# A mixture-of-experts decoder step on one core: routing moved into the experts' stage, slot tables built by matrix products

## What is computed

```
scores = sigmoid(x @ router_w)            # 1088 x 16 experts
sel    = scores + router_b                # chooses: best of 4 groups by the sum of its two best, then top 2 in it
wts    = scores[chosen two] / their sum
# the 2176 (token, expert) pairs are sorted by expert, each expert's list is padded to whole blocks of 128
for each block b (its expert e):          # at most 32 blocks
    xb  = h[tokens of the block]          # 128 x 1024; a padding row reads the zero row number 1088
    y_b = (silu(xb @ w_gate[e]) * (xb @ w_up[e])) @ w_down[e]    # 1024->512, 1024->512, 512->1024
out[token] = sum over its two experts of weight * its row of y_b
```

## Time and profile before

| | |
|---|---|
| median of three executions | 2949.96 us (2946.91 to 2951.17) |
| the profiled execution's own time | 2947.33 us |
| its span, first to last instruction | 2945.7 us |
| PE busy | 2368.8 us, 80% |
| DVE busy | 1385.9 us, 47% |
| ACT busy | 1038.2 us, 35% |
| POOL busy | 369.9 us, 13% |
| mean granted PE clock | 0.889 of full speed |

### The profile page before, as it was taken

How to read it: one execution, slowest core, us unless ns; L and a number is a source line. 1 busy time by engine, 2 the same in 40 slices (tenths; PEclk the granted TensorE clock), 3 DMA queues, 4 the chain that set the end, 5 groups by cost and what they waited for, 6 DMA issues and landing times. The chain is left out here.

```text
span 2945.7 us, 40501 instructions
## 1 busy us (share of the span) xinstructions
PE 2368.8 (80%) x11677; PEld 1773.0 (60%) x11677; DVE 1385.9 (47%) x2304; ACT 1038.2 (35%) x1710; POOL 369.9 (13%) x441
## 2 busy tenths in 40 slices
PE   2999993875871999999698999999968439999950
PEld 0866662654751778888386666555657327778840
DVE  2411104454653575666383333433346627755647
ACT  1211111332211565655342333443322026655632
POOL 0000000360002100000010223000000031000115
PEclk9899996687875999999897999999978669999985
DMA  6165650662012786877543543223140039866854
GB/s 239 51 223 199 219 193 27 170 188 105 29 37 96 260 308 234 294 255 269 188 151 135 177 140 134 93 82 118 51 169 29 29 136 338 309 236 228 315 188 153
DMA packets 196247, 500.28 MB, mean 170 GB/s; under 512 B 22323, under 2 KB 42036, under 8 KB 189654
## 3 DMA queue, kind: packets, MB, share of 16 engines
q1 hardware_dynamic: 164838, 403.70, 40.0%
q0 software_dynamic: 21776, 66.25, 6.7%
q10 hardware_dynamic: 9536, 29.13, 2.5%
HBM read 433.38 MB, written 68.83 MB: 170 GB/s over the span
## 5 line engine op out<-in xcount | busy, mean ns | idle before, releaser
L1880 DVE TENSOR_TENSOR e_wl<-e_raw,e_wh 128x1024 fp32r<-128x1024 f32 x384 | 449.3, 1219 | 174.2 <-ACT e_wh L1793 174.2
L1793 ACT CAST e_wh<-e_raw 128x1024 fp32r<-128x1024 f32 x384 | 382.6, 1050 | 208.1 <-SPq L1665 149.5
L1725 PE MATMUL e_psG<-e_wh,e_xh 128*128 128x512 f32 x784 | 321.2, 410 | 14.8 <-DVE e_xl L1894 7.5
L1726 PE MATMUL e_psG<-e_wl,e_xh 128*128 128x512 f32 x784 | 312.4, 398 | 0.0
L1727 PE MATMUL e_psG<-e_wh,e_xl 128*128 128x512 f32 x784 | 312.1, 398 | 0.0
L1725 PEld LDWEIGHTS e_psG<-e_wh,e_xh 128*128 128x128 f32 x784 | 149.1, 190 | 48.0 <-DVE e_xl L1894 8.3
L311 PE MATMUL in_ps<-in_w_upper,in_h_upper 128*128 128x512 f32 (+1 forms) x432 | 177.1, 410 | 0.0
L312 PE MATMUL in_ps<-in_w_lower,in_h_upper 128*128 128x512 f32 (+1 forms) x432 | 171.4, 397 | 0.0
L313 PE MATMUL in_ps<-in_w_upper,in_h_lower 128*128 128x512 f32 (+1 forms) x432 | 170.8, 395 | 0.0
L1727 PEld LDWEIGHTS e_psG<-e_wh,e_xl 128*128 128x128 f32 x784 | 148.9, 190 | 36.0
L1725 PE MATMUL e_psY<-e_wh,e_hh 128*128 128x512 f32 x392 | 158.1, 403 | 13.9 <-DVE e_hl L1903 13.9
(11 more groups left out here) (489 smaller groups left out, 4382.3 us busy)
## 6 DMA issues: line engine op xcount, KB each, us to landing
e_raw<-in_e_gate SPq DMA_DIRECT2D x32, 2048.0 KB
e_raw<-in_e_up SPq DMA_DIRECT2D x32, 2048.0 KB, 8.8
e_raw<-in_e_down SPq DMA_DIRECT2D x32, 2048.0 KB, 8.1
x<-in_ada_w SPq DMA_DIRECT2D x40, 1024.0 KB, 5.5
yrows<-e_y ACTq DMA_DIRECT2D x49, 512.0 KB, 7.2
x<-in_cache SPq DMA_DIRECT2D x64, 320.0 KB, 3.4
a_pages<-in_cache SPq DMA_DIRECT2D x64, 320.0 KB, 3.4
in_w_raw<-in_a_w_in POOLq DMA_DIRECT2D x48, 256.0 KB, 4.4
```

Source lines behind the costliest of these rows:

```text
L1725: T.matmul(out, upper[:, k, :], wh[:, z, cols], start=k == 0, stop=False)
L1726: T.matmul(out, upper[:, k, :], wl[:, z, cols], start=False, stop=False)
L1793: S.copy(wh[:, z, c * PC:(c + 1) * PC], raw[:, z, c * PC:(c + 1) * PC]).then_inc(s_hi[z], 1)
L1880: V.tensor_tensor(wl[:, z, at], raw[:, z, at], wh[:, z, at].bitcast(F32), ALU.subtract).then_inc(s_lo[z], 1)
```

## The change

`stage_route` is gone; its work is done at the head of `stage_experts`, by the same engines. In parts:

1. SP loads the bias and a constant `counts` (128 x 137 floats: the numbers 0 to 127, and each token's number minus 1088), and at once the three matrices of expert 0 of the layer. The table for later loads is waited for after that (`s_tab`).
2. The number of blocks of expert 0 is raised to at least 1, so that slot 0 is always expert 0's.
3. ACT's `upper(UP, 0)` stands before `copy_x(0)`, `copy_x(1)`.
4. DVE's chain is cut in `choose`, `weigh`, `count` and `tables`. The weights are computed after the masks are given to PE. The slot tables are computed after the row numbers.
5. `slot_token`, its filling with "no token" and the 18 scatters are gone. In their place `count` splits each destination into slot (shift by 7) and row (and 127), makes for each choice a mask of 128 x (9 x 32) and one of 128 x (9 x 128), multiplies the first by the token's number minus 1088, and PE sums 18 products (128 x 128 by 128 x 32) into `psH`: entry (row, slot) is the token number minus 1088, or 0. DVE adds 1088 and writes the whole numbers `tokens`.
6. POOL gathers slot 0 with the first column of `tokens`. In the loop a copy on POOL moves column b+1 into `tok` in place of the DMA from DRAM; it stands before the wait for the transposes, and the gather after it.
7. The scratch tiles of routing lie in the place of `wl`; one stage boundary for each layer is gone.

```diff
-def stage_route(nc, g, layer):
...
-            for k in range(2):
-                for t in range(TILES):
-                    r = rows_of(t)
-                    nc.gpsimd.indirect_dma_start(
-                        g.slot_token, bass.IndirectOffsetOnAxis(g.dest[0:r, k, t:t + 1], axis=0),
-                        ids[0:r, t:t + 1], None).then_inc(s_sc, 16)
...
 def stage_experts(nc, g, layer):
...
-            first = table(sp, g.slot_expert, 0) + layer * E
+            sp.dma_start(rb[:], g.router_b.broadcast_to([P, E])).then_inc(s_ld, 16)
+            sp.dma_start(counts[:], g.const["counts"]).then_inc(s_ld, 16)
+
             for z in range(3):
-                fetch(z, first)
+                fetch(z, layer * E)
+            sp.wait_ge(s_tab, 1)
             load(GATE, 1)
...
         def _(po):
-            def gather(b):
-                po.dma_start(tok[:], g.slot_token[bass.ds(b * P, P), :]).then_inc(s_tok, 16)
-                po.wait_ge(s_tok, 16 * b + 16)
+            def gather(rows):
+                nc.gpsimd.indirect_dma_start(xg[:], None, g.h2, bass.IndirectOffsetOnAxis(rows, axis=0)
+                                             ).then_inc(s_x, 16)
+
+            po.wait_ge(s_tok, 1)
+            gather(tokens[:, 0:1])
+            po.wait_ge(s_tab, 1)
+
+            def slot(b):
+                po.wait_ge(s_x, 16 * b + 16)
+                nc.gpsimd.tensor_copy(tok[:], tokens[:, bass.ds(b + 1, 1)])
+                po.drain()
+                po.wait_ge(s_xt, b + 1)
                 po.sem_inc(s_ask, 1)
...
+                gather(tok[:])
...
         def _(pe):
...
+            pe.wait_ge(s_oh, 1)
+            b2 = both[:].rearrange("p t e -> p (t e)")
+            T.matmul(psY[:, 0, 0:TILES * E], g.tri[:, 2, :], b2, start=True, stop=True)
+            T.matmul(psY[:, 1, 0:TILES * E], g.ones[:], b2, start=True, stop=True).then_inc(s_cnt, 1)
+
+            for k in range(2):
+                pe.wait_ge(s_hot, k + 1)
+                for t in range(TILES):
+                    mm = T.matmul(psH[:, 0, 0:SLOTS], hot_row[:, k, t, :], hot_slot[:, k, t, :],
+                                  start=(k == 0 and t == 0), stop=(k == 1 and t == TILES - 1))
+            mm.then_inc(s_num, 1)
             turn_x(0)
             gate(0, 0)
             gate(0, 1)
+            pe.wait_ge(s_tab, 1)
...
+            S.activation(sc[:], g.logits[:], ACT.Exp, scale=-1.0).then_inc(s_e, 1)
             upper(GATE, 0)
+            upper(UP, 0)
             act.wait_ge(s_xt, 1)
             copy_x(0)
             copy_x(1)
-            upper(UP, 0)
             silu(0)
+            act.wait_ge(s_tab, 1)
...
+            def count():
+                v.wait_ge(s_cnt, 1)
...
+                V.tensor_scalar(blocks[:, 0:1], blocks[:, 0:1], 1.0, None, ALU.max)
...
+                V.memset(destf[NSAMP:P, :, TILES - 1:TILES], float(2 * SLOTS * P))
+                v.drain()
+                V.tensor_copy(desti[:], destf[:])
+                v.drain()
+                places = desti[:].rearrange("p k t -> p (k t)")
+                V.tensor_scalar(parti[:, 0, :], places, 7, None, ALU.arith_shift_right)
+                V.tensor_scalar(parti[:, 1, :], places, P - 1, None, ALU.bitwise_and)
+                v.drain()
+                V.tensor_copy(partf[:], parti[:])
+                v.drain()
+                ids = counts[:, P:P + TILES].unsqueeze(2).broadcast_to([P, TILES, SLOTS])
+                for k in range(2):
+                    slot_of, row_of = (partf[:, j, k * TILES:(k + 1) * TILES] for j in range(2))
+                    V.tensor_tensor(hot_slot[:, k, :, :], counts[:, 0:SLOTS].unsqueeze(1).broadcast_to([P, TILES, SLOTS]),
+                                    wide(slot_of, SLOTS), ALU.is_equal)
+                    V.tensor_tensor(hot_row[:, k, :, :], counts[:, 0:P].unsqueeze(1).broadcast_to([P, TILES, P]),
+                                    wide(row_of, P), ALU.is_equal)
+                    v.drain()
+                    V.tensor_tensor(hot_slot[:, k, :, :], hot_slot[:, k, :, :], ids, ALU.mult)
+                    v.drain()
+                    v.sem_inc(s_hot, 1)
+                return a
...
+            choose()
+            weigh()
+            a = count()
+            V.tensor_tensor(full[:], ends[:, a, :].unsqueeze(1).broadcast_to([P, TABLE, E]),
+                            g.count_up[:].unsqueeze(2).broadcast_to([P, TABLE, E]), ALU.is_le)
+            v.drain()
+            v.wait_ge(s_num, 1)
+            V.tensor_scalar(tokens[:], psH[:, 0, 0:SLOTS], float(N), None, ALU.add).then_inc(s_tok, 1)
+            V.tensor_reduce(slotf[:], full[:], AX, ALU.add)
+            v.drain()
+            tables(a)
             lower(GATE, 0)
             lower_x(0, 0)
             lower_x(0, 1)
```

More of the change, by code:

```diff
@@ L1 @@
 from contextlib import ExitStack
+import math
 import numpy as np
@@ L1391, in _ @@
             v.sem_inc(s_z, 1)
-def stage_route(nc, g, layer):
[L1398 to L1456, removed]
-            for k in range(2):
-                for t in range(TILES):
-                    r = rows_of(t)
-                    nc.gpsimd.indirect_dma_start(
-                        g.slot_token, bass.IndirectOffsetOnAxis(g.dest[0:r, k, t:t + 1], axis=0),
-                        ids[0:r, t:t + 1], None).then_inc(s_sc, 16)
[L1463 to L1556, removed]
-                V.tensor_copy(ends[:, 1 - a, 0:k], ends[:, a, 0:k])
-                v.drain()
-                a, k = 1 - a, 2 * k
-            V.tensor_tensor(tmp[:], ends[:, a, :], blocks[:], ALU.subtract)
-            V.tensor_tensor(full[:], ends[:, a, :].unsqueeze(1).broadcast_to([P, TABLE, E]),
-                            g.count_up[:].unsqueeze(2).broadcast_to([P, TABLE, E]), ALU.is_le)
-            v.drain()
-            V.tensor_reduce(slotf[:], full[:], AX, ALU.add)
-            V.tensor_scalar(tmp[:], tmp[:], float(P), None, ALU.mult)
-            v.drain()
-            V.tensor_scalar(slotf[:], slotf[:], float(E - 1), None, ALU.min)
-            V.tensor_tensor(place[:], carry[:, 0:TILES, :], tmp[:].unsqueeze(1).broadcast_to(sh3), ALU.add)
-            v.drain()
-            V.tensor_copy(g.slot_expert[:], slotf[:])
-            V.memset(fresh[:, 0:1], 1.0)
-            V.tensor_tensor(fresh[:, 1:], slotf[:, 1:], slotf[:, 0:TABLE - 1], ALU.is_gt)
-            V.tensor_tensor(taken[:], ends[:, a, E - 1:E].broadcast_to([P, TABLE]), g.count_up[:], ALU.is_gt)
-            V.tensor_copy(g.slots_used[:], ends[:, a, E - 1:E])
-            v.drain()
-            V.tensor_tensor(fresh[:], fresh[:], taken[:], ALU.mult)
-            v.drain()
-            V.tensor_copy(g.slot_fresh[:], fresh[:])
-            V.tensor_tensor(place[:], place[:], ps[:, 0, 0:TILES * E].rearrange("p (t e) -> p t e", e=E), ALU.add)
-            v.drain()
-            for k in range(2):
-                V.tensor_tensor(work[:], place[:], oh[k][:], ALU.mult)
-                v.drain()
-                V.tensor_reduce(destf[:, k, :], work[:], AX, ALU.add)
-                v.drain()
-            V.tensor_copy(g.dest[:], destf[:])
-            v.drain()
-            v.sem_inc(s_dest, 1)
@@ L1627, in stage_experts, with scratch @@
         s_tok, s_ask, s_x, s_xt, s_xh, s_xl, s_xu = (sem(n) for n in (
-            "tokens_loaded", "tokens_known", "rows_gathered", "rows_turned", "xT_upper", "xT_lower", "xT_half_used"))
+            "tokens_ready", "rows_asked", "rows_gathered", "rows_turned", "xT_upper", "xT_lower", "xT_half_used"))
         s_silu, s_hid, s_ht, s_hh, s_hl, s_out, s_st, s_fill, s_end = (sem(n) for n in (
             "silu_ready", "hidden_ready", "hidden_turned", "hT_upper", "hT_lower", "y_out", "y_stored", "unused_filled", "passed"))
+        s_ld, s_e, s_oh, s_cnt, s_hot, s_num, s_tab = (sem(x) for x in (
+            "side_loaded", "exp_ready", "choices", "counted", "places_ready", "tokens_summed", "tables_ready"))
         block = ctx.enter_context(nc.Block())
         GATE, UP, DOWN = range(3)
+        at = [routing_at]
+        def scratch(n, shape, d=F32):
+            t = nc.alloc_sbuf_tensor_at(f"e{layer}_{n}", shape, d, offset=at[0])
+            at[0] += -(-math.prod(shape[1:]) * 4 // 32) * 32
+            return t
+        sh3 = [P, TILES, E]
+        rb, counts = scratch("bias", [P, E]), scratch("counts", [P, P + TILES])
+        sc, sel, work = scratch("scores", sh3), scratch("sel", sh3), scratch("work", sh3)
+        oh = [scratch("first", sh3), scratch("second", sh3)]
+        gs, gm, gi = (scratch(n, [P, TILES, GROUPS]) for n in ("gs", "gm", "gi"))
+        pr = scratch("pairs", [P, TILES, GROUPS, 3])
+        mx, ws = scratch("mx", [P, TILES]), scratch("ws", [P, TILES])
+        both, tot, place = scratch("both", sh3), scratch("tot", sh3), scratch("place", sh3)
+        carry = scratch("carry", [P, TILES + 1, E])
+        more = scratch("more", [P, E, TILES])
+        blocks, ends, tmp = scratch("blocks", [P, E]), scratch("ends", [P, 2, E]), scratch("start", [P, E])
```

(33 more changed lines are left out.)

108 lines of the change are left out of this document (92 added, 16 removed).

## The result

The changed kernel takes 2902.61 us (median of four, 2899.05 to 2908.49) against 2950.02 before: 0.9843 of it, 95% interval 0.9824 to 0.9862. The gain is 47 us where 61 were forecast. The profiled execution took 2899.05 us and its span is 2897.4, 48.3 less than before.

What follows compares the result with a forecast made beforehand. PE bounds the expert loops; a serial routing chain bounds the hole ahead of each. Savings of 29.5 and 32.6 us make 62.1, less 1 for fetches: 61, so 2949.96 - 61 = 2889 us, 8 in 10 within 2880 to 2899.

Steps and rivals of the forecast that it cites:

- the shorter holes: From routing's start to the first gate product: 41.4 us in each layer, saving 29.5 and 32.6, together 62.1.
- DVE's terms: DVE's routing chain: counting 7.7 us, parts 1.0, masks 4.8, with 1.2 won at the copy of the totals.
- masks of 1152 columns: DVE's larger masks in routing: 1.35 us each, by a straight line through rows of other sizes.
- the signal to PE: In layer 0's routing, DVE's signal comes at 893.4 in place of 895.56, as the weights move behind it.
- the covered counting products: DVE's weights, some 2.3 us, cover PE's two counting products in routing, for which DVE had idled 1.47 us.
- a gather 4.3 to landing: Slot 0's gather in routing, with the matrices already landed: priced at 4.4 us from issue to landing.
- expert 0 has a slot: The clamp to one block adds no slot, since every expert already had one in each layer.
- In the loop ... I cost it at nothing: POOL's one-column copy replaces the row numbers' DMA in each slot; PE never waits for a gather: 0 us.
- the loop gains too: Rival, 7%: earlier gathers and 49 fewer small loads remove PE's waits for up matrices; 2870 at best, 2879 if half.
- New on PE ... 2.2: Row-number products in routing: 18 instructions per nine at 0.12 us; first nine hidden under masks, last nine cost 2.2.
- the case that I had put at 4.4 more: Row-number products at double price: last nine 2.2 us later, first nine stick out too, 4.4 in all.
- Fetches: DVE's instruction fetches beside matrix loads: 0.5 us a layer taken; rival, 13%: up to 10 a layer, 2894 to 2909.
- The slower rival: Rival, 2%: POOL's copy waits for DVE in every slot, making gathers late; slower beyond 10.2 us of delay, 2988 at 11.

Runs made afterwards that it cites:

- e2: The kernel before, with slot b+1's row numbers loaded ahead of the wait for the transposes, so the gather starts early; 2971.74 us, 1.0061 of before.
- e1: The changed kernel, with POOL's gather in the loop held until DVE has multiplied the previous slot's hidden tile; 2892.45 us, 0.979 of before.
- e5: The changed kernel with its loop gather late and PE kept busy in routing by 46, 18 and 5 unread products; 2879.44 us, 0.9757 of before.
- e4: The changed kernel, with expert 0's three matrices asked for only when the slot tables are ready; 2939.53 us, 0.9947 of before.
- e3: The changed kernel, with 30, 16 and 5 unread products of ones put on PE in routing; 2908.91 us, 0.9849 of before.
- e9: The changed kernel with its loop gather late, masks in fp32r and PE kept busy by 46, 18 and 5 unread products; 2876.98 us, 0.9728 of before.

## Why the prediction was wrong

The way was right, and so was the mechanism of the gain (the shorter holes), with DVE's terms to a tenth: masks of 1152 columns 1.35 us, the last mask's end 29.7 us after the start as forecast, the signal to PE and the covered counting products as forecast, a gather 4.3 to landing, expert 0 has a slot. Of 61 us, 48.3 are there by the profiled executions, 47.4 by the medians. The difference by steps:

- **"In the loop ... I cost it at nothing": 11.0 us, the step that failed.** I asked whether PE would wait for the gather, which became earlier and could only be less late. The question was what an earlier gather runs into. It shares the DMA engines with the up matrix, the one transfer that the loop already waited for the earlier trace rows. e2 makes this loss alone on the old kernel (18.6 us in the loops), e1 takes it away from the new one (16.8), so it is shown. I had seen only PE's possible wait for the gather, and held that nothing in the loop can be late as long as PE bounds it. I had the mechanism in the prediction, as an argument against the rival "the loop gains too", and did not price it as a loss.
- **"New on PE ... 2.2": mis-sized, 0.22 us an instruction, not 0.12.** The row that I took the earlier trace rows is a shape match, but it stood behind a hundred microseconds in which PE was busy 85 to 94% of the time, at a granted clock of 0.82 to 0.91, and it ran at full clock itself: the first stretch below is its own. In routing PE has idled, and runs at half:

```profile
859.00:863.00 4.00, 2.63 (x23) 2.29 (x20) 0.00 (x0) 1.23 (x3) 0.00 (x0) 1.00 0.26 90
```

```profile
907.90:916.00 8.10, 7.89 (x36) 7.76 (x36) 3.03 (x5) 0.00 (x0) 0.00 (x0) 0.50 0.00 0
```

  The first nine products then stick out from under DVE's masks (the case that I had put at 4.4 more). The row numbers came 3.3 us later than forecast; POOL answered 0.6 sooner, the gather landed 0.1 sooner and x was split 0.5 sooner than I allowed, and the holes are 2.1 and 2.2 us longer than forecast, 4.3 in all. e5 shows the clock as the cause.
- **Fetches**: 1 us taken, none seen beyond what was there before. DVE's stop is 0.41 us beside the loading matrices (DMA share 1.05), 0.46 before in quiet DMA; that either of them is a fetch isn't shown. That rival is out: no stop on DVE got longer beside the matrices, which agrees with the page's "mostly hidden" (the Trainium skill, Runtime: NRT & Kernel Launch, Instruction fetch mechanics) for straight code.
- **Rest**: the stretches that nothing touched moved by -1.5 us here, by more in other executions; the median of after lies 3.6 over its profiled execution, which was the fastest of four.
- The slower rival's mechanism, POOL's copy waiting for DVE (the Trainium skill, SBUF — State Buffer, Terms), never cost PE anything: the copy took 0.2 to 1.3 us, the longest by about one DVE instruction of 1.2 us more than the shortest, which agrees with that page, and the transposes did not wait for a gather in the loop.

The sum: -62.1 + 4.3 + 11.0 - 1.5 = -48.3.

## What to carry to other kernels

A transfer that comes sooner is not free even where nothing waits for it: look up which other transfer is in flight at its new time, and whether that one has a waiter; then start the one with slack behind it. Price a matrix product by a row at the clock that its new place will have: look at the granted clock of the row's stretch, and at what PE did ahead of the new place. An early load and an order that relies on it belong together; where the load may be late, the order costs (some 5 us here, by the estimate at e4).

## What the runs showed of the hardware

- Small fp32 products (128x128 by 128x32) cost 0.12 us an instruction at granted clock 1.00 and 0.22 at 0.50, two instructions each; stored as fp32r they are one instruction of 0.23 at 0.50.
- In e3 PE worked 8 us without a gap and then stood idle for 4.27 us; the granted clock was 0.66 over the 4 us in which it resumed and 0.50 over the next 4. Without the hole it stayed at 1.00 (e5). In e9, layer 0, it was 0.60 over the 4 us from a gap of 0.95 us on.
- So a wait in the loop costs PE more than the wait: behind one of 2.68 us products of 512 columns took 0.63 us for about 3 us, in place of 0.40.
- A gather of 128 rows of 4 KB landed 4.3 us after its issue with no matrix in flight (slot 0 of layer 0). Over all gathers of the changed kernel, many of which go out beside a 2 MB matrix, it took 9.2 us in the middle and 10.7 at most. Where ACT waited for an up matrix in the loops, it began 0.8 us later than in the kernel before, on the mean (12.5 us after the issue, not 11.7).
- Keeping PE busy with products that nobody reads, 69 of them a layer, took the median from 2889 to 2879 us; 7.5 us of it are seen in the holes.
